# The gate's input slots and the output slots of a state-space mixer as three float32r products, in a one-core kernel of two model blocks

## The reference, cut to what matters

```
h = modulate(rmsnorm(x), shift, scale)
z, xBC, dt = h @ w_in            # w_in: 1024 x (2048 + 3072 + 32)
xBC = silu(causal_conv4(xBC))    # x: 2048 channels, B and C: 512 each
y = scan(x, B, C, softplus(dt + dt_bias), -exp(a_log)) + d * x
y = y * silu(z)                  # the gate
y = groupwise_rmsnorm(y) * gate_norm     # 4 groups of 512 channels
x = x + gate * (y @ w_out)       # w_out: 2048 x 1024
```

## Time and profile before

| | |
|---|---|
| runs (3) | 2889.53, 2890.04, 2892.01 us |
| median | 2890.04 us |
| span of the profiled execution | 2890.3 us |
| the profiled execution's own time | not recorded apart from its span |
| PE busy | 2770.7 us, 96% |
| DVE, ACT, POOL busy | 1186.3, 709.9, 48.3 us |
| mean DMA rate | 238 GB/s |
| mean granted TensorE clock | 0.976 of 2.4 GHz |

### The profile page before, as it was taken

How to read it: one execution, slowest core, us unless ns; L and a number is a source line. 1 busy time by engine, 2 the same in 40 slices (tenths; PEclk the granted TensorE clock), 3 DMA queues, 4 the chain that set the end, 5 groups by cost and what they waited for, 6 DMA issues and landing times.

```text
span 2890.3 us, 49935 instructions
## 1 busy us (share of the span) xinstructions
PE 2770.7 (96%) x22276; PEld 1973.5 (68%) x22276; DVE 1186.3 (41%) x2055; ACT 709.9 (25%) x1136; POOL 48.3 (2%) x39
## 2 busy tenths in 40 slices
PE   8899999999999999999998999999999999998998
PEld 6788997877533333333332756899999965697998
DVE  4667764332301101101101587356555433553554
ACT  2234333131200000000000214334444322211443
POOL 0000000000000000000000000000000000131000
PEclk9899999999999999999999999999999998999999
DMA  8756765544899999999999225265554330010452
GB/s 334 304 182 260 277 259 204 190 175 150 347 373 421 421 420 421 420 421 420 421 412 421 74 97 193 73 262 204 190 182 160 140 117 15 24 54 24 181 184 80
DMA packets 95198, 686.88 MB, mean 238 GB/s; under 512 B 10624, under 2 KB 11776, under 8 KB 11904
## 3 DMA queue, kind: packets, MB, share of 16 engines
q1 hardware_dynamic: 94400, 681.37, 60.5%
q10 hardware_dynamic: 576, 2.25, 0.2%
HBM read 682.52 MB, written 1.05 MB: 237 GB/s over the span
## 4 chain that ended last, share of the span: by engine, by line
PE 86%; DMA 6%; DVE 5%; ACT 2%; issue 1%; SPq 0%; POOL 0%; ACTq 0%; DVEq 0%
PE ps L530 42%; PE ps L2053 15%; PE ps L890 12%; PE ps L801 6%; PE ps L2078 5%; DMA AR<-W 3%; DMA ring<-W 2%; PE ps L543 2%; PE ps L2081 2%; PE ps L776 1%; PE ps L2061 1%; DVE macc L646 0%; DMA XT<-XIN 0%; SPq L3577 0%; ACT AR L1761 0%
## 5 line engine op out<-in xcount | busy, mean ns | idle before, releaser
L2053 PE MATMUL ps<-AR 128*32 128x512 f32 x2904 | 440.1, 593 | 11.6 <-DMA AR<-W 10.2
L530 PE MATMUL ps<-HT,ring 128*128 128x256 f32 (+1 forms) x1696 | 443.4, 422 | 1.7 <-ACT HT L719 1.7
L530 PEld LDWEIGHTS ps<-HT,ring 128*128 128x128 f32 x1696 | 324.2, 193 | 114.5 <-issue 75.0
L530 PE MATMUL ps<-FR,FR 128*128 128x256 f32 x3120 | 387.4, 284 | 0.0
L530 PEld LDWEIGHTS ps<-FR,FR 128*128 128x128 f32 x3120 | 378.7, 192 | 3.0 <-issue 2.9
L872 DVE TENSOR_TENSOR FR<-ring,FR 128x2048 fp32r<-128x2048 f32 x129 | 294.4, 2291 | 164.4 <-ACT FR L856 164.4
L890 PE MATMUL ps<-FR,FR 128*128 128x256 f32 x2832 | 349.0, 283 | 0.0
L890 PEld LDWEIGHTS ps<-FR,FR 128*128 128x128 f32 x2832 | 343.8, 192 | 0.0
L2173 DVE TENSOR_TENSOR AR<-AR,ps 128x256 f32<-128x256 f32 x70 | 29.6, 423 | 678.9 <-ACT AR L2136 361.0
L2053 PE MATMUL ps<-ring,AR 128*32 128x512 f32 x1576 | 288.8, 594 | 5.8 <-DMA ring<-W 3.5
L856 ACT ACTIVATE FR<-ring 128x2048 fp32r<-128x2048 f32 x129 | 244.7, 1908 | 130.9 <-PE ps L890 85.2
(11 more groups left out here) (430 smaller groups left out, 2517.1 us busy)
## 6 DMA issues: line engine op xcount, KB each, us to landing
ring<-W SPq DMA_DIRECT2D x431, 1024.0 KB, 5.8
AR<-W SPq DMA_DIRECT2D x215, 1024.0 KB, 21.0
XT<-XIN ACTq DMA_DIRECT2D x2, 1024.0 KB, 8.7
cst<-CS SPq DMA_DIRECT2D x1, 1859.0 KB, 14.3
out<-XT SPq DMA_DIRECT2D x4, 256.0 KB, 2.2
sml<-SM SPq DMA_DIRECT2D x1, 970.5 KB, 10.3
cst<-CS ACTq DMA_DIRECT2D x1, 129.5 KB, 8.1
sml<-SM ACTq DMA_DIRECT2D x1, 16.0 KB, 5.7
```

The lines of the kernel that those rows point to most:

```text
L530: ins = g.matmul(out, l, r, **kw)
L2053: ins = g.matmul(bank.ap[group(i), :], mo.hg[e % 2][:, 4 * h + k, group(t)], w[n][:, k, :], start=j == 0 and k == 0, stop=j == 1 and k == ...
```

## The change

Eight input slots (`ssm_in` 13 to 20, the gate) and six output slots (`ssm_out` 2 to 7) are computed as three float32r products. A class `InPlace` makes the parts without buffers of its own: the high part of slot i (counted over the 14) goes to memory that is dead at that time (for even i the cells of B and C, for odd i below 8 the cells of the scan's `E`, for odd i from 9 on `raw`), the low part over the weights in the ring slot itself. So the next high part but one waits until the slot is used. The input's parts go to the second half of `HT` and to `sq`; high parts of the gated outputs 4 to 15 go over z, low parts over the outputs themselves. The parts of a slot are made two slots ahead of PE in the projections. In the output stage the order on DVE is written anew, the reciprocal of group 3 moves ahead, and the modulation steps move: on PE from behind slots 0, 2, 3, 4, 5, 6 to behind 1 to 6, in the order of loads from behind slots 0 to 5 to behind 2 to 7, on DVE from one run of six at the end to places between the new work.

```diff
@@ schedule
     for i in range(8):
         load("ssm_out")
-        bg.go(i < 6)
+        bg.go(i >= 2)
@@ after Splits
+        class InPlace(Splits):
+            def pair(self, i):
+                return self.hi(i)[0], ring_low[:, where[slot(*self.names[i])][0], :]
+            def make_act(self, g, s, n):
+                while self.made < n:
+                    i = self.made
+                    src, wait, _ = self.get(*self.names[i])
+                    wait(s)
+                    for one in self.hi(i)[1]:
+                        s.wait_ge(*one)
+                    g.activation(self.pair(i)[0], src, ACT.Copy).then_inc(*s.done(self.x + ".hi", i))
+                    self.made += 1
+            def make_dve(self, g, s, n):
+                while self.made < n:
+                    i = self.made
+                    src, wait, _ = self.get(*self.names[i])
+                    high, low = self.pair(i)
+                    wait(s)
+                    s.wait_ge(self.x + ".hi", i)
+                    g.tensor_tensor(low, src, high.bitcast(F32), SUB).then_inc(*s.done(self.x + ".lo", i))
+                    self.made += 1
@@ the mixer's stage
+        ma.names = [("ssm_in", n_) for n_ in range(13, 21)] + [("ssm_out", n_) for n_ in range(2, 8)]
+        def split_hi(i):
+            if i % 2 == 0:
+                return ma.low[:, 8192:10240], [("ma.cb_ps", 3) if i == 0 else split_used(i - 2)]
+            if i < 8:
+                return ma.low[:, e_at:e_at + 2048], [split_used(i - 2)] if i > 1 else []
+            return ma.low[:, raw_at:raw_at + 2048], [split_used(i - 2) if i > 9 else ("ma.cv", conv_tiles(12)[1], 2)]
+        def split_used(i):
+            return ("ma.in", 13 + i) if i < 8 else ("ma.used", i)
@@ mamba_pe
+            def project3(n):
+                b = counts.take("ma.in", n)
+                s.wait_emptied(b).wait_ge("ma.hlo").wait_ge("ma.lo", n - 13)
+                for h in range(2):
+                    ins = up3(g, w.pair(n - 13), (ma.hhi, ma.hlo), h * 128, b.ap[:, h * 256:h * 256 + 256])
+                ins.then_inc(*s.done("ma.in", n, frees=(slot("ssm_in", n),)))
+                bg.go(ssm_steps(n))
+            def down_split(i, acc):
+                v = [x.rearrange("p (k c) -> p k c", k=2) for x in w.pair(i + 6)]
+                s.wait_ge("ma.ylo", 2 * i + 1).wait_ge("ma.lo", i + 6)
+                for kk, m in down_order(i == 7):
+                    k, h = 2 * i + kk, m % 2
+                    for j, (l, r) in enumerate(three([x[:, kk, m * 128:m * 128 + 128] for x in v], [ma.yhi[:, k, :], ma.ylo[:, k, :]])):
+                        ins = g.matmul(acc[m // 2].ap[:, h * 256:h * 256 + 256], l, r, start=False, stop=i == 7 and kk == 1 and h == 1 and j == 2,
+                                       skip_group_check=True)
...
+                ins.then_inc(*s.done("ma.used", i + 6, frees=(slot("ssm_out", i),)))
             for n in range(13, 21):
-                project(n)
+                project3(n)
                 if n in (13, 15):
                     turned((n - 9) // 2)
@@ the output slots on PE
-                down_slot(g, s, "ma.down", "ssm_out", i, 8, acc, lambda k: ma.y[:, k, :], [("ma.g", 2 * i + 1)])
-                bg.go((1, 0, 1, 1, 1, 1, 1, 0)[i])
+                if i < 2:
+                    down_slot(g, s, "ma.down", "ssm_out", i, 8, acc, lambda k: ma.y[:, k, :], [("ma.g", 2 * i + 1)])
+                else:
+                    down_split(i, acc)
+                bg.go((0, 1, 1, 1, 1, 1, 1, 0)[i])
@@ mamba_act, slots 1 to 12
+                if n == 9:
+                    g.activation(ma.hhi, HT[:, :, 0:256], ACT.Copy).then_inc(*s.done("ma.hhi"))
+                if n >= 11:
+                    w.make_act(g, s, n - 10)
@@ slots 13 to 20, behind the wait for the slot and ahead of silu of z
+                w.make_act(g, s, min(j + 3, 8))
@@ behind the last squares
+            w.make_act(g, s, 10)
             root_act(g, s, "ma.rms3", 13, 2, 512)
+            for k in range(4, 16):
+                s.wait_ge("ma.g", k)
+                g.activation(ma.yhi[:, k, :], ma.y[:, k, :], ACT.Copy).then_inc(*s.done("ma.yhi", k))
+            w.make_act(g, s, 14)
@@ mamba_dve, at the head of slot n; and behind the convolution
+                if n >= 13:
+                    w.make_dve(g, s, min(n - 10, 8))
...
+                if n == 10:
+                    s.wait_ge("ma.hhi")
+                    g.tensor_tensor(ma.hlo, HT[:, :, 0:256], ma.hhi.bitcast(F32), SUB).then_inc(*s.done("ma.hlo"))
+                if 11 <= n <= 12:
+                    w.make_dve(g, s, n - 10)
@@ gated and the end
+            def low(q):
+                for k in range(4 * q, 4 * q + 4):
+                    s.wait_ge("ma.yhi", k)
+                    g.tensor_tensor(ma.ylo[:, k, :], ma.y[:, k, :], ma.yhi[:, k, :].bitcast(F32), SUB).then_inc(*s.done("ma.ylo", k))
             def gated(q):
-                if q == 3:
-                    rstd_dve(g, s, "ma.rms3", 13, 2)
...
-            for q in range(4):
-                gated(q)
-            bg.go(6)
-            residual_dve(g, s, "ma.down", ("down", "ma.down", 7), MN["ssm_mod"][0], 16)
+            gated(0)
+            w.make_dve(g, s, 10)
+            gated(1)
+            rstd_dve(g, s, "ma.rms3", 13, 2)
+            low(1)
+            bg.go()
+            gated(2)
+            gated(3)
+            low(2)
+            low(3)
+            for n in range(11, 15):
+                bg.go()
+                w.make_dve(g, s, n)
+            bg.go()
+            residual_dve(g, s, "ma.down", ("ma.used", 13), MN["ssm_mod"][0], 16)
```

More of the change, by code:

```diff
@@ L451, in program @@
         so, nsm = offsets(SMALL)
+        with ExitStack() as first:
+            ring_low = first.enter_context(nc.sbuf_tensor("ring_low", [128, RING, SLOT], F32R))
         ring = sb("ring", [128, RING, SLOT])
@@ L455, in program @@
         XT = sb("XT", [128, 2, 8, 256])
+        with ExitStack() as first:
+            HT_low = first.enter_context(nc.sbuf_tensor("HT_low", [128, 8, 512], F32R))
         HT = sb("HT", [128, 8, 512])
@@ L1544, in program @@
         m_ = memory(3, 25500, (384,))
+        with ExitStack() as first:
+            ma.low = first.enter_context(nc.sbuf_tensor("ma_low", [128, 25500], F32R))
         ma.fr = m_.fr[0]
+        ma.yhi = ma.low[:, 0:4096].rearrange("p (k t) -> p k t", k=16)
+        ma.ylo = ma.low[:, 4096:8192].rearrange("p (k t) -> p k t", k=16)
         ma.z = m_.get(4096, "p (k t) -> p k t", k=16)
         ma.cv = m_.get(6144, "p (k t) -> p k t", k=24)
+        raw_at = m_.at
         ma.raw = m_.get(8 * 259, "p (k t) -> p k t", k=8)
@@ L1559, in program @@
         ma.cb = m_.get(4 * 384, "p (g c) -> p g c", g=4)
+        e_at = m_.at
         ma.E = [m_.get(384) for _ in range(8)]
+        ma.hlo = ma.low[:, m_.at:m_.at + 2048].rearrange("p (k t) -> p k t", k=8)
+        ma.hhi = HT_low[:, :, 256:512]
         ma.sq = m_.get(8 * 256, "p (k t) -> p k t", k=8)
         ma.y = ma.cv[:, 0:16, :]
+        ma.names = [("ssm_in", n_) for n_ in range(13, 21)] + [("ssm_out", n_) for n_ in range(2, 8)]
[7 more added lines that the diff above has]
+            return ("ma.in", 13 + i) if i < 8 else ("ma.used", i)
         def conv_tiles(n):
@@ L1581, in project @@
                 bg.go(ssm_steps(n))
+            w = InPlace("ma", ma.names, split_hi, split_used, from_ring)
+            def project3(n):
[13 more added lines that the diff above has]
+                                       skip_group_check=True)
+                    if i == 7 and kk == 1 and m in (1, 3, 5):
+                        ins.then_inc(*s.done("two", "ma.down", m // 2))
+                ins.then_inc(*s.done("ma.used", i + 6, frees=(slot("ssm_out", i),)))
             def turned(n):
```

4 lines of the change are left out of this document (added).

## The result

| | median | lowest to highest | executions |
|---|---|---|---|
| kernel before | 2890.04 us | 2885.41 to 2892.01 | 5 |
| changed kernel | 2868.52 us | 2865.13 to 2873.97 | 5 |

The ratio is 0.9928 (95% interval 0.9916 to 0.9939): 21.5 us faster. The forecast was 2872.1 us with a range from 2869.5 to 2879.0. The profiled execution took 2865.13 us with a span of 2863.1 us.

What follows compares the result with a forecast made beforehand. PE was taken to bound the mixer, loads the expert stage behind it. Projections 9.2, outputs 6.9 and the wait 1.8 made 17.9 us saved: 2890.04 - 17.9 = 2872.1 us, range 2869.5 to 2879.

Steps and rivals of the forecast that it cites:

- the wait for the reciprocal: Output stretch: PE waits 1.82 us for DVE's reciprocal of the last group's root; moved ahead, 1.8 us saved.
- the price of a slot's products: Each of 14 mixer slots: 48 float32r records at 5.86 us instead of 7.01, saving 1.15 us a slot, 16.1 us.
- lower bound of 5.77: Slot price from MLP products behind other float32r work: 5.77 us, 17.4 us saved in all.
- The extra load: Expert stage: 11 loads instead of 10 follow the mixer's end; bounds 0 and 2.5 us lost, taken as 0.
- the mixer ends 18 us earlier while the expert stage ends only 15 us earlier: Sign of being wrong: the expert stage does not end as much earlier as the mixer, 15 against 18 us.
- rival 3: Mixer slots: products closer together, by rows at most 5.77 us a slot, giving 2870.8 us; chance 0.02.
- The second pair: Projections: second slot's high and low parts, ready near 559.9, wanted by PE at 561.6; spare 1.7 us, the narrowest place.
- The second spare: Ring loads: beyond landing 1.0 us before ACT wants them, another 2.3 us before PE feels a late load.
- 1 (new waits): Projection or output slots: new waits cost 1 us at each of eight or six, about 2879 us; chance 0.15.
- 2 (the extra load in full): Load-bound expert stage takes the one extra load in full: 2.5 us lost, 2874.6 us; chance 0.15.
- 4 (landing chain): Projections: load landings set the period, slower from landings of 10.5 us on; about 2904 us at 12.7; chance 0.04.
- 5 (clock): Changed slots: gaps lower PE's clock, products taking about twice as long at 1.2 GHz; no separate chance beyond new waits.

Runs made afterwards that it cites:

- p_output_slots: Changed kernel with the eight gate slots as before; only output slots 2 to 7 in float32r, new orders kept: 2881.11 us, ratio 0.9960 to the kernel before.
- o_loads: Changed kernel with loads issued in the order PE uses them, modulations behind output slots 1 to 6 instead of 2 to 7: 2873.48 us, ratio 0.9931.
- x_more_dve: Changed kernel plus two dummy DVE subtractions behind each ring subtraction of slots 15 to 20, ahead of the modulation's row copy: 2878.69 us, ratio 0.9952.
- c_again: The changed kernel run a second time, nothing altered: 2873.79 us, ratio 0.9934 to the kernel before.

## Why the prediction was right, and where it was not

**The bound and the mechanism: right.** PE carried the chain; fourteen slots got shorter, the wait for the reciprocal went, and the loads of the next stage started as much earlier.

**The failed step is the price of a slot's products**, "Every changed slot has f32 work before it, so I take 5.86". The form of the sum was right, and this term of it was mis-sized: 5.76 us were measured (595.44 to 601.20). The first records of such a slot, in the MLP of the kernel before and in the changed mixer, show which half of the argument failed (PE's timelines; the first start of the MLP's slot is 1892.14):

```profile
1892.37 0.40 PE L530 MATMUL ps<-FR,FR 128*128 128x256 f32 x2
```

```profile
595.44 0.39 PE L534 MATMUL ps<-HT_low,ma_low 128*128 128x256 f32 x1
595.67 0.28 PE L534 MATMUL ps<-ma_low 128*128 128x256 f32 x1
```

Behind a modulation step the first record takes 0.23 us to the start of the next in both (1892.14 to 1892.37 and 595.44 to 595.67), where behind float32r work it takes 0.12. That is the 0.1 us between 5.86 and 5.77, and it came as argued. What did not carry over is the spacing of the other 47: 5.63 us in the MLP (1892.37 to 1898.00), 120 ns each, and 5.53 us in the mixer (595.67 to 601.20), 117.7 ns each. That the sum falls on the lower bound of 5.77 is chance; that bound stood for another case. The saving is 1.25 us instead of 1.15 a slot (8.44 - 7.19), 1.4 us over 14. The wait gave 2.1 us instead of 1.8. Together 19.6 us instead of 17.9.

The rule of the Trainium skill that had been weighed (TensorE: Matmul & The Clock Gate, Back-to-back issue gap; 109 ns for an isolated warm matmul of 256 columns) would have a slot at 5.24 us, an estimate. The rows show 117.7 ns, nearer to it than the MLP's 120, but they still disagree with it.

**The extra load: right.** It went into idle time: p_output_slots has it and its products part is 830.60 us, o_loads has it not and its is 831.79. **The expert stage: missed.** It is 2.1 us longer in the changed kernel (1.9 to 2.5 in its three profiles), in two of them in part by the clock and for the rest for a reason that is not the load and that I have not found. The prediction had "the mixer ends 18 us earlier while the expert stage ends only 15 us earlier" as a sign of being wrong; the profiled execution has 23.2 and 21.2 us. The sum by stretches is 10.0 + 9.6 - 2.1 = 17.5 us; the scan is 0.7 to 1.0 us shorter and P was another 1.6 us shorter in two of three profiles, both where the clock fell less. All 16 executions of the changed kernel have a median of 2872.0 us and all 58 of the kernel before 2891.4: 19.4 us. The three separate comparisons gave 21.5, 18.1 and 20.0.

**The range: too narrow at the low end.** It is said to end at 5.77 us slots, but those give 2870.8 us (rival 3); its end of 2869.5 lies 1.3 us further and 2.6 us under the forecast. That leaves next to nothing for the scatter of the measurement itself, since three runs within 2.5 us seemed to show none. Over many executions the standard deviation is 3.1 us (before) and 3.6 us (changed). A median of five scatters by about 2 us from that alone (an estimate: 1.25 times 3.6, over the root of 5), for both kernels. The forecast of 2872.1 is where the 16 executions lie, and that is luck in part: 1.7 us too little for slots and wait stands against some 2 us lost in the expert stage that it did not have. The first five executions lay 3.5 us lower.

**The spare times.** The second pair, the narrowest place by the forecast, had 1.5 to 1.6 us (1.7 forecast). From the third pair on, the pairs had 2.2 to 5.0 us (4.2 forecast) and the row copies 0.4 to 3.2 (2.3 forecast), so the narrowest place was not the one named. The loads were said to land 1.0 us ahead of ACT. That was wrong: with a median landing of 6.2 us instead of 4.9, ACT's copies start 0.7 to 2.1 us after PE has freed the place, and at five slots in a row they wait for a landing. The second spare, "another 2.3 us before PE feels it", covered that with 0.4 us left. The median from the old pace, one load per 4.2 us, did not hold at the new one, one per 3.6 us; why landings take longer there was not tried.

**The rivals.** 1 (new waits) did not come; x_more_dve shows its place. 2 (the extra load in full) had the size of what X lost but not its cause: o_loads took the load away and X stayed. 3 (products closer together) is what happened by rows, at 5.76; I had given it 0.02 because I took the MLP's price for the mixer's. 4 (landing chain) would need landings of 10.5 us; the median was 6.2. 5 (clock): 1.00 in both stretches.

## What to carry to other kernels

Where PE sets the chain and ACT and DVE stand idle beside it, three float32r products are worth 1.25 us for each f32 slot of 16 products here, and the parts need no buffers of their own if the high part has dead cells and the low part overwrites the weights. What must be checked is each in-order queue that the new work enters: a small copy that PE waits for belongs ahead of a large subtraction that itself waits for a load. Its spare has to be taken at the narrowest slot, not at a typical one. And a difference of a few microseconds is better read from the length of a stretch that PE fills (O repeats to 0.02 us) than from whole executions that scatter by 10 us or more. A stretch with waits in it, as P or X, has to be compared at an equal clock. The range of a forecast must hold that scatter.

## What the runs showed of the hardware that had not been expected

**Closer spacing than in the MLP.** The same three products with the same shapes lie 117.7 ns apart here and 120 there. The rate of the loads beside them is not the cause: in the MLP the spacing is the same at 424 GB/s (1892.14 to 1898.00) and at 270 (1898.00 to 1903.77), and the mixer's stretch had 267. Operands and their buffers differ; which of it matters was not tried.

**Steps of 1.6 us in code that is the same.** P is 96.9 or 98.5 us in the same kernel. The timelines of PE show one origin, right behind its wait for DVE before the B and C products. The changed kernel:

```profile
516.92 1.57 PE L534 MATMUL ps<-AR 128*128 128x256 f32 x8 [2.54 <-DVE AR L1888]
518.33 7.07 PE L534 MATMUL ps<-HT,ring 128*128 128x256 f32 x32
525.24 0.50 PE L534 MATMUL ps<-cst,mrow 128*128 128x2 f32 x4
```

c_again, the same code:

```profile
517.59 2.89 PE L534 MATMUL ps<-AR 128*128 128x256 f32 x8 [2.54 <-DVE AR L1888]
520.27 7.47 PE L534 MATMUL ps<-HT,ring 128*128 128x256 f32 x32
527.58 0.50 PE L534 MATMUL ps<-cst,mrow 128*128 128x2 f32 x4
```

The windows of the 8 records, from start to start, in the same order:

```profile
516.92:518.33 1.41, 1.41 (x8) 1.31 (x9) 1.33 (x3) 0.00 (x0) 0.00 (x0) 1.00 0.20 81
```

```profile
517.59:520.27 2.68, 2.68 (x8) 2.31 (x9) 1.43 (x3) 0.00 (x0) 0.00 (x0) 0.51 0.10 43
```

After an equal wait of 2.54 us the 8 records run at a granted clock of 1.00 once and of 0.51 the other time, the upper level (2.4 GHz) and, but for the edge of the window, the lower one (1.2 GHz). They take 1.41 us and 2.68 us, and the next 32 take 0.4 us more: 8.32 us against 9.99 from the end of the wait to the sums, 1.67 us. The clock fell there in nine of the 13 profiled executions, in both of the kernel before and in one of three of the changed kernel. A kernel of this length has several such waits, which is one source of the scatter: of the first five executions of the changed kernel the fastest (2865.13 us) has a mean clock of 0.979 and the slowest (2873.97) one of 0.975.

**A load-bound stage that is not quite fixed.** With the same code in it, the products part of the expert stage takes 830.6 to 833.1 us, and the 22.5 to 24.1 us behind it go with the clock. Neither the order of the loads ahead of the stage nor the windows of its DMA rate explain the products part.
